# Two attention mixers with their groups in another order, one engine's low halves a step later, and all block copies on ScalarE

## The reference

```
h = rms_norm(x) @ w_in                      # 2916 columns: cq, ckv, kr, fox, moba, diff, mem_q
o_a = attention(mla q, k, v)                # q, k from low-rank cq, ckv; normed and rotated
o_b = attention(norm(q), norm(k), v, decay) # "fox"
o_c = attention(rope(norm(q)), rope(norm(k)), v)          # "moba"; with 256 tokens one causal block
o_d = norm((softmax(q1 k1) - lam * softmax(q2 k2)) @ v)   # "diff": two softmaxes, one set of values
o_e = attention(norm(q), memory k, memory v)              # "memq", not causal
x = x + concat(o_a .. o_e) @ w_o            # 1280 rows
```

## Time and profile before

| | |
|---|---|
| median of three runs | 1662.05 us |
| the profiled execution | 1665.06 us |
| its span, first to last instruction | 1663.8 us |
| mean granted TensorE clock | 0.947 |
| TensorE busy | 1504.5 us (90%) |
| VectorE busy | 1062.7 us (64%) |
| ScalarE busy | 741.0 us (45%) |

### The profile page before, as it was taken

How to read it: one execution, slowest core, us unless ns; L and a number is a source line. 1 busy time by engine, 2 the same in 40 slices (tenths; PEclk the granted TensorE clock), 3 DMA queues, 4 the chain that set the end, 5 groups by cost and what they waited for, 6 DMA issues and landing times. The chain is left out here.

```text
span 1663.8 us, 26062 instructions
## 1 busy us (share of the span) xinstructions
PE 1504.5 (90%) x10862; PEld 1419.4 (85%) x10862; DVE 1062.7 (64%) x1533; ACT 741.0 (45%) x1151; POOL 190.5 (11%) x164
## 2 busy tenths in 40 slices
PE   6877987999998787999999969899999978899999
PEld 5865877999997577999997759799999767899999
DVE  4653547765467846665467775577766776577763
ACT  5322324444346434444345545444445554454443
POOL 0002332110000002110001200010100110010100
PEclk9888988999999989999999988899999997899999
DMA  7431303555544323655544321255565421145563
GB/s 236 129 100 51 102 1 115 165 185 190 184 153 154 124 77 102 196 183 178 190 161 156 125 76 48 80 195 181 175 202 178 153 76 48 59 145 182 173 199 105
DMA packets 186389, 230.07 MB, mean 138 GB/s; under 512 B 5920, under 2 KB 161056, under 8 KB 186016
## 3 DMA queue, kind: packets, MB, share of 16 engines
q1 hardware_dynamic: 185264, 221.99, 41.3%
q0 software_dynamic: 1008, 6.41, 1.1%
HBM read 227.34 MB, written 1.05 MB: 137 GB/s over the span
## 5 line engine op out<-in xcount | busy, mean ns | idle before, releaser
L766 DVE TENSOR_TENSOR weights_low<-weights_raw,weights_high 128x1024 fp32r<-128x1024 f32 (+3 forms) x421 | 509.7, 1231 | 363.3 <-ACT weights_high L664 362.8
L664 ACT CAST weights_high<-weights_raw 128x1024 fp32r<-128x1024 f32 (+3 forms) x421 | 424.3, 1030 | 325.3 <-PE bank L493 323.3
L491 PE MATMUL bank<-hT_high,weights_high 128*128 128x256 f32 (+1 forms) x1672 | 487.5, 292 | 39.3 <-DVE hT_low L849 21.5
L492 PE MATMUL bank<-hT_low,weights_high 128*128 128x256 f32 (+1 forms) x1672 | 482.7, 289 | 0.0
L493 PE MATMUL bank<-hT_high,weights_low 128*128 128x256 f32 (+1 forms) x1672 | 482.2, 288 | 0.0
L491 PEld LDWEIGHTS bank<-hT_high,weights_high 128*128 128x128 f32 (+1 forms) x1672 | 330.3, 198 | 47.0 <-issue 30.2
L492 PEld LDWEIGHTS bank<-hT_low,weights_high 128*128 128x128 f32 (+1 forms) x1672 | 330.1, 197 | 0.4
L493 PEld LDWEIGHTS bank<-hT_high,weights_low 128*128 128x128 f32 (+1 forms) x1672 | 329.7, 197 | 0.4
L491 PE MATMUL bank<-aT_high,weights_high 128*128 128x256 f32 x864 | 241.8, 280 | 0.2
L492 PE MATMUL bank<-aT_low,weights_high 128*128 128x256 f32 x864 | 241.6, 280 | 0.0
L493 PE MATMUL bank<-aT_high,weights_low 128*128 128x256 f32 x864 | 241.2, 279 | 0.0
(11 more groups left out here) (409 smaller groups left out, 1928.5 us busy)
## 6 DMA issues: line engine op xcount, KB each, us to landing
weights_raw<-in_w_up SPq DMA_DIRECT2D x32, 1024.0 KB, 5.3
weights_raw<-in_w_down SPq DMA_DIRECT2D x32, 1024.0 KB, 5.0
weights_raw<-in_ffn_w_gate SPq DMA_DIRECT2D x22, 1024.0 KB, 5.2
weights_raw<-in_ffn_w_up SPq DMA_DIRECT2D x22, 1024.0 KB, 5.2
weights_raw<-in_w_in SPq DMA_DIRECT2D x20, 1024.0 KB, 5.0
weights_raw<-in_w_in_ab SPq DMA_DIRECT2D x16, 1024.0 KB, 5.7
weights_raw<-in_ffn_w_down SPq DMA_DIRECT2D x16, 1024.0 KB, 5.0
weights_raw<-in_w_o SPq DMA_DIRECT2D x10, 1024.0 KB, 5.5
```

Of the source, the lines that this page charges most:

```text
L491: k.E.matmul(out, xh, wh, start=first, stop=False)
L492: k.E.matmul(out, xh, wl, start=False, stop=False)
L664: k.A.copy(w.halves(n)[0], w.raw_part(n)).then_inc(*k.s.weight_high(n))
L766: k.V.tensor_tensor(low, w.raw_part(n), high.bitcast(F32), ALU.subtract).then_inc(*k.s.weight_low(n))
```

## The change

Five edits, all in the two mixers of the second stack:

1. The groups stand in the order fox, mla, diff, diff, moba, memq. Their norms, rotations, squares, waits and the panels of `w_o` move along (`OUT_2`). The two diff groups now use `QK` slot 0, and so does moba after them.
2. `last_columns` of VectorE: the rotation of mla comes ahead of the low half of its stop, and the later low halves come one stop after ScalarE's high halves.
3. `last_columns` of ScalarE: panel 2048 is emptied one stop earlier, ahead of the copies of mla's q and k.
4. `copies_by_scalar`: ScalarE makes all copies to `QK` and `PT` (15 a mixer were VectorE's).
5. The root for the norm of diff falls in step 6 instead of step 7, because its group stands one place earlier.

```diff
-OUT_2 = [2, 0, 4, 6, 8]
+OUT_2 = [2, 0, 6, 4, 8]
...
     def by_scalar(self, n, block):
-        return (n + block) % 2 == 0
+        return self.copies_by_scalar or (n + block) % 2 == 0
...
@@ scalar_heads_turned
-    for c in range(0, g.blocks, 4):
+    for c in range(0, g.blocks, 2 if a.copies_by_scalar else 4):
@@ vector_attention
-        if not a.groups[n].shared:
+        if not a.groups[n].shared and not a.copies_by_scalar:
             vector_heads_turned(k, a, n)
@@ attention_2
-        Group(4, P, in_pairs, 64 ** -0.5, True, values(C_MOBA + 512), out(2), mask=cneg),
         Group(4, P, in_fours(0), 32 ** -0.5, True, values(C_DIFF + 512), None, mask=cneg),
-        Group(4, P, in_fours(1), 32 ** -0.5, True, values(C_DIFF + 512), out(3), mask=cneg, shared=True),
+        Group(4, P, in_fours(1), 32 ** -0.5, True, values(C_DIFF + 512), out(2), mask=cneg, shared=True),
+        Group(4, P, in_pairs, 64 ** -0.5, True, values(C_MOBA + 512), out(3), mask=cneg),
@@ scalar_mixer_2
         scalar_split(k, n2 + 1)
-        yield
         for t in range(NT):
             evacuated(2048, t)
+        yield
         scalar_split(k, n2 + 4)
...
     def finish(n):
-        if n == 4:
+        if n == 3:
             scalar_root(k, (st, "sub"), m.st2[:, :, 0:4])
@@ vector_mixer_2
+        mla_turned()
         vector_split(k, n2 + 1)
-        mla_turned()
         yield
         vector_split(k, n2 + 4)
-        for i in range(1, 5):
-            yield
-            vector_split(k, n5 + i)
+        yield
+        yield
+        vector_split(k, n5 + 1)
+        yield
+        vector_split(k, n5 + 2)
+        yield
+        vector_split(k, n5 + 4)
...
     def work(n):
         if n == 2:
+            squared(DIFF)
+            scaled(DIFF)
+            turned_heads("diff", C_DIFF, 16, 32, ROT_D, ROT_C + ROT_A + ROT_M)
+        elif n == 4:
             squared(MOBA)
             scaled(MOBA)
             turned_heads("moba", C_MOBA, 8, 64, ROT_M, ROT_C + ROT_A)
```

More of the change, by code:

```diff
@@ L1813, with __init__ @@
 class Attention:
-    def __init__(self, st, m, groups, slots, key, out):
-        self.st, self.m, self.groups, self.slots, self.key, self.out = st, m, groups, slots, key, out
+    def __init__(self, st, m, groups, slots, key, out, copies_by_scalar=False):
+        self.st, self.m, self.groups, self.slots, self.key, self.out, self.copies_by_scalar = st, m, groups, slots, key, out, copies_by_scalar
         self.slot = []
@@ L2205 @@
 SLOT = {"cq": 0, "ckv": 1, "kr": 2, "fox": 3, "moba": 11, "diff": 19, "memq": 35}
-SQUARED = ["memk", "cq", "ckv", "kr", "fox", "mla_q", "mla_kv", "moba", "diff", "memq"]
+SQUARED = ["memk", "cq", "ckv", "kr", "fox", "mla_q", "mla_kv", "diff", "moba", "memq"]
 def attention_2(k, l):
@@ L2224, in attention_2 @@
         Group(8, 96, lambda hh: (hh, 0, 96), 96 ** -0.5, True, lambda hh, u: m.kva[:, u, hh * P + 64:(hh + 1) * P], out(1), mask=cneg),
-        Group(4, P, in_pairs, 64 ** -0.5, True, values(C_MOBA + 512), out(2), mask=cneg),
         Group(4, P, in_fours(0), 32 ** -0.5, True, values(C_DIFF + 512), None, mask=cneg),
-        Group(4, P, in_fours(1), 32 ** -0.5, True, values(C_DIFF + 512), out(3), mask=cneg, shared=True),
+        Group(4, P, in_fours(1), 32 ** -0.5, True, values(C_DIFF + 512), out(2), mask=cneg, shared=True),
+        Group(4, P, in_pairs, 64 ** -0.5, True, values(C_MOBA + 512), out(3), mask=cneg),
         Group(4, P, in_pairs, 64 ** -0.5, False, lambda hh, u: kvm[:, u, 256 + hh * 64:256 + (hh + 1) * 64], out(4)),
     ]
-    return Attention(("m2", l), m, groups, 1, ("o_2", l), m.out)
+    return Attention(("m2", l), m, groups, 1, ("o_2", l), m.out, copies_by_scalar=True)
 def projected_to(k, l, end):
@@ L2287, in tensor_mixer_2 @@
         lambda c, t: (qa4 if c < 4 else ka4)[:, t, c % 4, :],
-        lambda c, t: m.hp[:, t, C_MOBA + c * P:C_MOBA + (c + 1) * P],
         lambda c, t: m.hp[:, t, C_DIFF + c * P:C_DIFF + (c + 1) * P],
         None,
+        lambda c, t: m.hp[:, t, C_MOBA + c * P:C_MOBA + (c + 1) * P],
         lambda c, t: m.hp[:, t, C_MEM + c * P:C_MEM + (c + 1) * P] if c < 2 else kvm[:, t, (c - 2) * P:(c - 1) * P],
@@ L2302, in prepare @@
         elif n == 2:
+            E.wait_ge(*s.turned.at((l, "diff", 1)))
+        elif n == 4:
             E.wait_ge(*s.turned.at((l, "moba", 1)))
-            for mark in projected_to(k, l, 2048):
+            for mark in projected_to(k, l, D_IN2):
                 E.wait_ge(*mark)
-        elif n == 3:
-            E.wait_ge(*s.turned.at((l, "diff", 1)))
         else:
@@ L2378, in work @@
         if n == 2:
+            roots("diff", 19, 16)
+        elif n == 4:
             roots("moba", 11, 8)
-        elif n == 3:
-            roots("diff", 19, 16)
         elif n == 5:
@@ L2544, in work @@
             turned_heads("moba", C_MOBA, 8, 64, ROT_M, ROT_C + ROT_A)
[L2545 to L2548, removed]
         elif n == 5:
@@ L2557, in finish @@
             V.wait_ge(*s.products.at(((st, "out T", before), "T", 0)))
-        if n == 3:
+        if n == 2:
             for hh in range(4):
@@ L2561, in finish @@
             vector_scaled(k, m.d1, bank, rden, k.banks.read(key))
-        elif n == 4:
+        elif n == 3:
             vector_scaled(k, m.d2, bank, rden, k.banks.read(key))
@@ L2565, in finish @@
             V.wait_ge(*s.lam.at((l, "minus")))
-            V.wait_ge(*k.banks.was_read((st, "values", 3)))
+            V.wait_ge(*k.banks.was_read((st, "values", 2)))
             then(V.scalar_tensor_tensor(m.d1, m.d2, m.lm[:, 66:67], m.d1, ALU.mult, ALU.add))
@@ L2574, in finish @@
             then(last)
-            V.scalar_tensor_tensor(a.groups[4].out[0], m.d1, 1.0 - lam_init, spread(row("sub"), 1, NT), ALU.mult, ALU.mult
-                                   ).then_inc(*s.mixed((st, 4)))
+            V.scalar_tensor_tensor(a.groups[3].out[0], m.d1, 1.0 - lam_init, spread(row("sub"), 1, NT), ALU.mult, ALU.mult
+                                   ).then_inc(*s.mixed((st, 3)))
         else:
@@ L2610, in gpsimd_mixer_2 @@
         G.tensor_tensor(ka4[:, t, :, 32:96], ka4[:, t, :, 32:96], gk, ALU.mult).then_inc(*s.mla_gained((l, "k", t)))
-    for kind in (MOBA, DIFF, MEMQ):
+    for kind in (DIFF, MOBA, MEMQ):
         squared_columns(*kind)
```

## The result

The changed kernel took 1644.66 us (median of four runs, 1639.43 to 1646.29), the kernel before 1661.43 beside it: a ratio of 0.990, 95% interval 0.986 to 0.994. The forecast was 1644. The gain is 17 to 27 us.

The account below looks back on a forecast made before the run. TensorE's waits (22.4 us a mixer) and the half clock around them were taken as the bound. Two mixers at 1.4 + 8.1 - 0.65 gave 17.7 us off 1665.1, 1647.4 profiled, forecast 1644 against the runs; range 1630 to 1660.

Parts of the forecast that it names:

- the sum: Both mixers: twice 1.4 us of waiting plus 8.1 of clock less 0.65 for the load, 17.7 us gained.
- table load: Behind each mixer, line 737: the root needs a load of its own, 1.28 us, of which 0.65 is late.
- Steps 1 and 2: Start of mixer: waits of 2.9 and 1.3 us go, 2.8 for the block of diff replaces 2.7; 4.1 saved.
- Step 3: Scores of group 2: the 6.8 us wait at line 2073 goes; emptying panel 2560 costs 0.5 instead of 1.4.
- Step 4: Ahead of the first output panel: TensorE waits 7.9 us for two banks behind VectorE's block of moba; bounds 0 and 11.
- Rival C: Wait ahead of the first output panel stays small: 5 of 7.9 us and its slow stretch go; 1630 us, chance 0.20.
- Steps 5 to 7: Rest of mixer: waits of 1.2 us, 2.5, 4.6 for open exponentials and banks, and 1.5 ahead of the last panel.
- this open wait: Ahead of the turning of memq: exponentials not covered by an output panel, 3 to 4 us, a sign of being right.
- The clock: Each mixer: TensorE busy at half clock for 18 us, down from 35.9, in three places; 8.1 us gained.
- Rival A: Both mixers: the clock is not given back, gain only 2 x 0.75 us, so 1660 us; chance 0.20.
- Rival B: Half clock throughout the panel-free part near 1021 to 1041 and from 998 to 1016: slower, about 1673 us; chance 0.08.

Follow-up runs that it names:

- e8: The changed kernel run again with nothing altered: 1639.8 us against 1667.2 for the kernel before, ratio 0.984.
- e9: Kernel before with one edit, VectorE rotates mla ahead of the low half of its stop: 1655.4 us against 1667.2, ratio 0.995.
- e4: Changed kernel with VectorE's block of moba behind the values of group 1 and its root behind ScalarE's group 2 copies: 1641.0 us, ratio 0.988 to kernel before.
- e1: Kernel before with the new group order alone, including the earlier root of diff's norm: 1667.0 us against 1661.0, ratio 1.002.
- e3: Kernel before with all of the change except the new group order: 1645.7 us against 1661.0, ratio 0.990.
- e6: Changed kernel with VectorE's block of diff ahead of the three low halves: 1640.1 us against 1663.5 for the kernel before, ratio 0.986.

## Why the prediction was right

The time and the mechanism were right: waits that are fewer and closer together, and most of the gain from the clock. That the median of 1644.7 lies within 1 us of the forecast is in part luck, since the same kernel took 1639.8 in e8. From the first mixer to the end the trace gained 21.5 us where the sum had 17.7. For one mixer idle time fell by 4.0 us (1.4 forecast) and busy time by 9.4 and 8.4 (8.1 forecast), the table load cost nothing (0.65 forecast), and 2.1 were given back behind the mixer, which the sum did not have.

*Steps 1 and 2.* Right: the rotation begins with the end of the maxima (953.59 against 953.68), the 2.9 us are gone. The new wait for the block of diff was put at 2.8 and is 4.0: counted from the start of the mixer, which lies 2.3 us later in the new profile, the block ends 0.6 us later than worked out and TensorE is there 0.5 us earlier. So 2.9 us are saved here and not 4.1. The rotation of this step alone brings more than half of what the low halves bring (e9).

*Step 3.* Right. The wait at line 2073 ahead of the scores is gone; the 0.5 for the emptying of panel 2560 is 0.3 + 0.7.

*Step 4.* Right in place, releaser and size: 7.9 forecast, 7.6 measured. TensorE arrives 1.4 us later than worked out and VectorE's reading ends 1.1 later, so the two errors cancel. Rival C (this wait stays small) fell. Whether it would have brought its 14 us is not shown. In e4, where the wait is 1.0 us, the time fell by no more than 4 us, but e4 moves the block to a later place, where C has all of it early.

*Steps 5 to 7.* 1.2 for step 5 was 1.0, 2.5 for step 6 was 1.7, 4.6 for the exponentials and banks was 2.4: part of TensorE's work ahead of the exponentials ran at half clock, which shortens their wait. The forecast named this open wait, ahead of the turning of memq, as a sign at 3 to 4 us; that sign was missed. Together the waits are 19.1 us against 21.0.

*The clock.* 18 us busy at half clock forecast, 15.4 and 17.4 measured in the mixers, and 3.4 behind each that I had not expected: 18.8 and 20.8. By place, in the first mixer, 3, 5 and 10 us were forecast and 3.4, 3.3 and 8.7 measured. Rival A (not given back) fell. Rival B fell too: between 1023.93 and 1044.00, with no output panel, TensorE is at half clock for 6.7 of 16.0 us busy (3.4 to 1035.76, 3.3 from 1040.71), not throughout, and between 1005.10 and 1032.30 it is full, though 1009 to 1018 hold only transposes, scores and values. The argument against B had counted 28 transposes in the full stretch of the earlier trace rows from 1016.5 to 1054; there are 56, which makes it stronger. The two stretches of the changed kernel:

```profile
1005.10:1032.30 27.20, 24.47 (x200) 22.76 (x199) 14.76 (x29) 18.20 (x48) 0.00 (x0) 1.00 0.12 39
1023.93:1044.00 20.07, 16.04 (x105) 14.43 (x103) 13.48 (x23) 12.67 (x30) 0.00 (x0) 0.80 0.17 53
```

The rule that transposes do not keep the clock up (the Trainium skill, "TensorE: Matmul & The Clock Gate", Part 4: PE-mode transpose) is neither shown nor refuted by this: the slow stretches in steps 6 and 7 do stand where there is no panel, but each begins within or behind a wait too.

*Table load.* Wrong, and a fault of the working: 0.65 a mixer was counted as late because `factor` is. ScalarE does load (1.28 us) and `factor` is about 0.7 later:

```profile
1454.64 1.28 ACT L737 ACT_TABLE_LOAD   x1
1455.93 0.47 ACT L737 ACTIVATE factor<-bank,consts 128x256 f32<-128x256 f32 x1
```

But TensorE is busy for 46.88 of 46.88 us from 1473.12 and 1453.32 on in the two kernels. Nobody waited. The load itself is priced right: `factor` starts 1.29 us behind the load's start, and no further time shows.

*The parts.* The forecast did not say which edit brings the gain, and its working suggests the order (it removes 6.8 and 4.5). That reading is wrong by e1 and e3: the order moves these waits and makes new ones of no smaller sum. What it does win in the mixers, 2 to 3 us each by less time at half clock, the slow stretch behind them takes back at 1.5 us each, in part or in whole.

## What to carry over

When a long block on one engine stands ahead of a wait of another, moving the block can just move the wait: all three moves here (the order, e4, e6) gave most of it back a step later or at what was put behind. What paid were edits that fill a gap instead: work put into idle time of its own engine (the rotation ahead of a low half that was not ready yet), copies put on the less busy of two engines, and TensorE's turn put into a panel with its operands in a place of their own. Test such parts one by one, since a whole that comes out as forecast does not show which of them did it.

## What was not expected of the hardware

The clock record is not a function of the program. In e8, the changed kernel again, the first mixer has TensorE busy at half clock for 20.1 us, and a wait of 4.9 where the other execution had 15.4 and 7.6:

```profile
939.10:1060.15 121.05, 104.02 (x703) 94.26 (x702) 76.94 (x157) 68.26 (x165) 11.22 (x9) 0.89 0.24 82
```

Its length is the same (121.05 against 120.98). The 4.7 us more at half clock are 2.4 us more busy time, and the wait is 2.7 us shorter. TensorE at half clock ahead of a wait on VectorE cost nothing here, because the wait shrank by as much. So the two terms, waits and clock, are only worth adding up for stretches that TensorE itself bounds; the same holds for e6's second mixer, where the open exponentials cost 0.8 in place of 2.7 and 3.4 us more are busy at half clock.
